# Laying a kernel's input by features and crossing its first four weight units

## The reference, cut to what matters

```python
def first_block(x, w_in, ...):
    proj = x @ w_in[l]                      # (256 x 1024) @ (1024 x 2560)
    q, k, v, g, p = jnp.split(proj, [...])  # 512 columns each
    q = _rope(q...)                         # rotation by position, on GpSimd here
    k = _rope(k...) * (RET_HEAD_DIM ** -0.5)
    ret = _retention(q, k, v)
    ...
    pool = _pool_mixer(p, w_pool[l], pool_scale[l])
    mix = jnp.concatenate([ret, pool], axis=-1) @ w_out[l]
    x = _layernorm(DEEPNORM_ALPHA * x + mix, ln1_g[l], ln1_b[l])
    ffn = _conv_ffn(x, ...)                 # 1024 -> 2 x 2816 -> 1024
    x = _layernorm(DEEPNORM_ALPHA * x + ffn, ...)
```

## Time and profile before

| | |
|---|---|
| median of the runs | 1067.66 us (1067.63 to 1068.27, 3 runs) |
| the profiled execution's own time | 1067.39 us |
| its span in the trace | 1065.4 us |
| PE busy | 1057.5 us (99%), 5158 matmuls |
| DVE, ACT, POOL busy | 738.0 us (69%), 596.5 us (56%), 96.5 us (9%) |
| moved by DMA | 227.13 MB, 213 GB/s on average |
| granted TensorE clock | 0.999 of full speed |

### The profile page before, as it was taken

The page is one execution under the profiler, slowest core; times in us unless marked ns, Lnnn a source line. Parts: engine busy times, 40 slices in busy tenths (PEclk is TensorE's granted clock), DMA queues, the critical chain, the costliest instruction groups (busy, mean ns, idle before and its releaser), DMA issues.

```text
span 1065.4 us, 13290 instructions
## 1 busy us (share of the span) xinstructions
PE 1057.5 (99%) x5158; PEld 890.2 (84%) x5158; DVE 738.0 (69%) x868; ACT 596.5 (56%) x804; POOL 96.5 (9%) x73
## 2 busy tenths in 40 slices
PE   9999999999999999999999999999999999999997
PEld 7888888888888888888888888888989988888886
DVE  6668777875786766467986768657568665867642
ACT  6463776764485645558655545464256557655531
POOL 2800000000000000000545500010000000000000
PEclk9999999999999999999999999999999999999999
DMA  9855999986588876475457844466556346777741
GB/s 357 301 171 170 302 282 293 306 265 197 180 269 244 246 246 227 158 242 171 160 164 215 249 145 158 138 239 218 180 178 214 119 139 210 238 245 241 243 166 40
DMA packets 152974, 227.13 MB, mean 213 GB/s; under 512 B 9376, under 2 KB 96336, under 8 KB 152784
## 3 DMA queue, kind: packets, MB, share of 16 engines
q1 hardware_dynamic: 149488, 214.86, 62.5%
q0 software_dynamic: 3136, 11.23, 3.1%
q10 hardware_dynamic: 288, 0.20, 0.1%
HBM read 211.57 MB, written 14.68 MB: 212 GB/s over the span
## 4 chain that ended last, share of the span: by engine, by line
PE 93%; DVE 3%; ACT 2%; issue 1%; DMA 0%; DVEq 0%; SPq 0%; ACTq 0%
PE ps L778 22%; PE ps L780 22%; PE ps L779 22%; PE ps L817 5%; PE ps L815 5%; PE ps L816 5%; PE ps L912 2%; PE ps L1237 1%; PE ps L1236 1%; PE ps L1235 1%; PE ps L1112 1%; DVE rest L1916 1%; PE ps L875 1%; PE ps L873 1%; PE ps L874 1%
## 5 line engine op out<-in xcount | busy, mean ns | idle before, releaser
L1916 DVE TENSOR_TENSOR rest<-raw,high 128x2048 fp32r<-128x2048 f32 x131 | 307.3, 2362 | 83.3 <-ACT high L1354 82.8
L778 PE MATMUL ps<-high,xt_high 128*128 128x512 f32 x840 | 330.5, 393 | 0.0
L780 PE MATMUL ps<-high,xt_rest 128*128 128x512 f32 x840 | 327.1, 389 | 0.0
L779 PE MATMUL ps<-rest,xt_high 128*128 128x512 f32 x840 | 327.0, 389 | 0.0
L1354 ACT ACTIVATE high<-raw 128x2048 fp32r<-128x2048 f32 x131 | 248.2, 1913 | 60.7 <-DMA raw<-in_ffn_w_down_dram 32.6
L780 PEld LDWEIGHTS ps<-high,xt_rest 128*128 128x128 f32 x840 | 157.7, 188 | 33.2
L779 PEld LDWEIGHTS ps<-rest,xt_high 128*128 128x128 f32 x840 | 157.9, 188 | 31.4
L778 PEld LDWEIGHTS ps<-high,xt_high 128*128 128x128 f32 x840 | 157.8, 188 | 31.2
L1921 DVE SCALAR_TENSOR_TENSOR rest<-raw,wgain,high 128x512 fp32r<-128x512 f32 x176 | 119.0, 746 | 36.0 <-ACT high L1358 36.0
L1358 ACT ACTIVATE high<-raw,wgain 128x512 fp32r<-128x512 f32 x176 | 110.8, 716 | 9.8 <-DMA raw<-in_ffn_w_in_dram 9.8
L1616 ACT ACTIVATE act<-ps,recips 128x256 f32<-128x256 f32 x44 | 18.4, 470 | 85.1 <-PE ps L780 85.0
(11 more groups left out here) (371 smaller groups left out, 1480.1 us busy)
## 6 DMA issues: line engine op xcount, KB each, us to landing
raw<-in_w_in_dram SPq DMA_DIRECT2D x88, 512.0 KB, 4.4
raw<-in_ffn_w_in_dram SPq DMA_DIRECT2D x88, 512.0 KB, 4.9
raw<-in_w_up_dram SPq DMA_DIRECT2D x44, 512.0 KB, 5.3
raw<-in_ffn_w_down_dram SPq DMA_DIRECT2D x44, 512.0 KB, 4.4
raw<-in_w_down_dram SPq DMA_DIRECT2D x22, 512.0 KB, 5.1
raw<-in_w_out_dram SPq DMA_DIRECT2D x16, 512.0 KB, 4.4
raw<-in_w_mkv_dram SPq DMA_DIRECT2D x16, 512.0 KB, 4.7
gv_turned<-gv_blocked SPq DMA_DIRECT2D x11, 512.0 KB, 7.0
```

The lines of the kernel that those rows point to most:

```text
L778: pe.matmul(out, sh, wh, start=first, stop=False)
L779: pe.matmul(out, sh, wr, start=False, stop=False)
L780: mm = pe.matmul(out, sr, wh, start=False, stop=last)
L1916: vec.tensor_tensor(rest[:, slot, c], raw[:, slot, c], high[:, slot, c].bitcast(F32), ALU.subtract).then_inc(unit_rest, 1)
```

## The change

The input is also handed over by features (`x_t`), so PE's sixteen transposes, and the ACT and DVE instructions that took them, are gone: ACT and DVE now split `xt_raw` directly, in five parts. Units 0 to 3 of `win1` hold the q and k blocks crosswise: unit 0 is q's first half, unit 1 k's first half, unit 2 and 3 their second halves, in twelve pieces that PE takes alternately from q and k for features 0 to 511, then q's rest, then k's. All weights are laid out on the host so that each DMA reads one unbroken piece of HBM (4 KB per partition, 2 KB for the first eight pieces); what the kernel loads into the slots is the same. `x` by tokens is loaded once, after unit 9. GpSimd's rotation tables wait for the eighth piece, its other constants for unit 4. PE's warming matmuls are seven, on a smaller tile. ACT issues the first part of `x_t` in place of `ident`, which follows later.

```diff
-WARM = (6, 4)
+WARM = 7
+LEAD_UNITS = 4
+XT_PARTS = ((0, 1), (1, 2), (2, 4), (4, 6), (6, 8))
+LEAD_PIECES = tuple((j, k, k + 1) for k in range(4) for j in range(2)) + tuple((j, k, k + 2) for j in range(2) for k in (4, 6))
...
+        def piece(name, c0, c1):
+            return dram[name][P * c0:P * c1].rearrange("(p n) -> p n", p=P)
...
+            def load_lead():
+                for n, (j, k0, k1) in enumerate(LEAD_PIECES):
+                    u = 2 * (k0 // 4) + j
+                    c = slice((k0 % 4) * NB, ((k1 - 1) % 4 + 1) * NB)
+                    for part, (x0, _) in enumerate(XT_PARTS):
+                        if part and j == 0 and x0 == k0:
+                            load_xt(part)
+                    at = u * 4 * NB
+                    sync.dma_start(raw[:, u, c], piece("units", at + c.start, at + c.stop)).then_inc(lead_landed[n], 16)
...
+            for u in range(LEAD_UNITS, UNIT["end"]):
+                load(u)
+                if u == UNIT["wout1"] - 1:
+                    sync.dma_start(x[:, :, :], dram["x"].rearrange("(t p) c -> p t c", p=P)).then_inc(x_landed, 16)
...
-            pool.wait_ge(unit_landed[3], 32)
+            pool.wait_ge(lead_landed[7], 16)
             for t, src in ((ropec, "c_ropec"), (ropes, "c_ropes")):
                 pool.dma_start(t[:], dram[src]).then_inc(rope_landed, 16)
+            pool.wait_ge(unit_landed[LEAD_UNITS], 32)
             for t, src in ((window, "c_window"), (decay, "c_decay"), (small["pscale"], "pool_scale")):
...
-            input_transposes(0)
-            warm(WARM[1])
-            wait_taken(("x", 0))
...
+            for n, (j, k0, k1) in enumerate(LEAD_PIECES):
+                u = 2 * (k0 // 4) + j
...
+                if n == 0:
+                    pe.wait_ge(xt_first, 1)
+                    pe.wait_ge(lead_high, 1)
+                    for tt in range(TT):
+                        xh, _, wh, _, out = lead(0, tt)
+                        pe.matmul(out, xh, wh, start=True, stop=False)
+                pe.wait_ge(lead_rest, n + 1)
+                if j == 0:
+                    pe.wait_ge(xt_rests, [part for part, (x0, x1) in enumerate(XT_PARTS) if x0 <= k0 < x1][0] + 1)
+                for k in range(k0, k1):
+                    for tt in range(TT):
+                        xh, xr, wh, wr, out = lead(k, tt)
+                        if n:
+                            pe.matmul(out, xh, wh, start=(k == 0), stop=False)
+                        pe.matmul(out, xh, wr, start=False, stop=False)
+                        mm = pe.matmul(out, xr, wh, start=False, stop=(k == KC - 1))
+                if k1 % 4 == 0:
+                    mm.then_inc(unit_used, 1)
+            full_block("win1", 2)
...
-            act.dma_start(small["ident"][:, :], dram["c_ident"]).then_inc(ident_landed, 16)
+            act.dma_start(xt_raw[:, 0, :], piece("x_t", 0, S)).then_inc(xt_landed[0], 16)
...
+            for n, (j, k0, _) in enumerate(LEAD_PIECES):
+                for part, (x0, _) in enumerate(XT_PARTS):
+                    if part and j == 0 and x0 == k0:
+                        input_high(part)
+                weights_high(n)
+            act.dma_start(small["ident"][:, :], dram["c_ident"]).then_inc(ident_landed, 16)
+            split[0] = LEAD_UNITS
...
+            vec.wait_ge(xt_landed[0], 16)
+            vec.tensor_copy(xt_high[:, 0, :], xt_raw[:, 0, :]).then_inc(xt_first, 1)
+            input_rest(0)
...
             split_to(UNIT["up1"] + 2)
+            vec.wait_ge(x_landed, 16)
             half_stats("wout1", 0, 0)
```

More of the change, by code:

```diff
@@ L541, in load @@
                     sync.wait_ge(unit_used, u - SLOTS + 1)
-                for dst, src in parts(raw[:, slot, :]):
-                    sync.dma_start(dst, src).then_inc(unit_landed[slot], 16)
+                for n in range(2):
+                    c = slice(2 * n * NB, 2 * (n + 1) * NB)
+                    sync.dma_start(raw[:, slot, c], piece("units", u * 4 * NB + c.start, u * 4 * NB + c.stop)).then_inc(unit_landed[slot], 16)
                 turn_conv(u)
@@ L936, in warm @@
                 for _ in range(n):
[L937 removed]
+                    pe.matmul(ps[:, 7, :], warmth[:, :], warmth[:, :].unsqueeze(1).to_broadcast([P, 4, P]), start=True, stop=True)
             pe.wait_ge(sem("warm_ready"), 1)
[L940 to L945 removed]
@@ L947, in _ @@
-            input_transposes(0)
-            warm(WARM[1])
-            wait_taken(("x", 0))
-            for tt in range(TT):
-                for k, (sh, sr, c, out, first, last) in enumerate(chunk_products("win1", 0, 0, tt)):
-                    if tt == 0:
-                        pe.wait_ge(*((sem("lead_rest"), k + 1) if k < 3 else (unit_rest, 1)))
-                    if (tt, k) == (0, 2):
-                        input_transposes(2)
-                    if (tt, k) == (0, 3):
-                        input_transposes(1)
-                    if (tt, k) == (1, 0):
-                        wait_taken(("x", 2))
-                    if (tt, k) == (1, 1):
-                        input_transposes(3)
-                    wh, wr = high[:, 0, c:c + NB], rest[:, 0, c:c + NB]
-                    pe.matmul(out, sh, wh, start=first, stop=False)
-                    pe.matmul(out, sh, wr, start=False, stop=False)
-                    mm = pe.matmul(out, sr, wh, start=False, stop=last)
@@ L966, in _ @@
-            mm.then_inc(unit_used, 1)
-            wait_taken(("x", 1), ("x", 3))
-            tiles = [chunk_products("win1", 0, 1, tt) for tt in range(TT)]
-            for k in range(4):
-                pe.wait_ge(*((sem("lead_rest"), k + 4) if k < 3 else (unit_rest, 2)))
-                for tt in range(TT):
-                    sh, sr, c, out, first, last = tiles[tt][k]
-                    wh, wr = high[:, 1, c:c + NB], rest[:, 1, c:c + NB]
-                    pe.matmul(out, sh, wh, start=first, stop=False)
-                    pe.matmul(out, sh, wr, start=False, stop=False)
-                    mm = pe.matmul(out, sr, wh, start=False, stop=last)
@@ L2667, in _, with in_pieces @@
             assert split[0] == UNIT["end"]
+def in_pieces(rows, ends):
+    return np.concatenate([rows[:, a:b].ravel() for a, b in zip([0] + list(ends), ends)])
 def constants():
```

210 lines of the change are left out of this document (91 added, 119 removed).

## The result

| | before | after |
|---|---|---|
| median of the runs | 1067.74 us (1067.63 to 1068.27, 5 runs) | 1072.12 us (1071.13 to 1074.45, 5 runs) |
| the profiled execution's own time | 1067.39 us | 1074.45 us |
| its span | 1065.4 us | 1072.3 us |
| first product | 6.53 | 4.48 |
| unit 4 (block p) starts | 30.12 | 28.17 |

The ratio after to before is 1.0042, with a 95% interval of 1.003 to 1.0053: slower by over 0.2%, and outside the range of 1064.0 to 1069.0. Two things make reading this kernel's trace harder than the one of before. Its executions lie 3.3 us apart where those of before lie 0.6 apart, and the profiled one is the slowest of them, so the profile shows 7.1 us of loss where the medians show 4.4.

A forecast was written before the change was run, and what follows sets the result against it. PE, busy 99% of the span, was taken as the bound. The opening's 3.4 us, less a new 2.4 us wait for GpSimd's rotation before k, left 1.0 us gained: 1066.5 us, range 1064.0 to 1069.0.

The forecast's parts named there:

- The start: First product on PE at 4.4 instead of 6.53, with a stall of 0.5 us before the third product.
- The opening: PE's q and k blocks before unit 4: ready for unit 4 at 26.7 instead of 30.12, 3.4 us won.
- PE runs on: After the third product, each 256 KB piece needs less time on DMA, ACT and DVE than PE's 1.36 us.
- When the first rotation starts: GpSimd begins its large constants about 20.3, spends 2.3 us on four issues, and rotates from 22.6.
- The insertions: DVE rests falling into GpSimd's rotations: three (units 4, 5, 7) at 2.0 us each, second rotation ending at 46.3.
- the gap of the DMA issues: GpSimd's DMA issues between the two rotations, where unit 6's rest was to fall.
- the rests get in at each boundary: Rival on GpSimd's rotations: four insertions give 1068.8 us, five 1070.8; chance 0.17, of it 0.10 with five.
- the undisturbed 17.7: Both GpSimd rotations without insertions, the four DMA issues between them included, take 17.7 us.
- At nothing: The other weights' layout, `x` after unit 9 and the later `ident` cost nothing; no PE wait ends in a DMA.
- 1.0 early: PE's transposes of k: wanted at 43.9, allowed at 46.35 after a 2.4 us wait, instead of 47.34.

The follow-up runs named there:

- e1: After, with eighteen matmuls of 512 columns that nothing reads put on PE before the transposes of k: 1069.21 us.
- e3: After, with ACT making the high part of unit 4 before it takes block q: 1069.78 us.
- e6: After, with the rests of units 4 to 8 computed on 512 of 2048 columns and the others set to zero by memset: 1069.6 us.
- e4: After, with GpSimd issuing the four small constants behind the rotation's tables instead of between its two rotations: 1070.61 us.
- e5: After once more, on another chip and with no edit: 1071.09 us.
- e9: After with the crossing undone, units 0 and 1 as q's halves and 2 and 3 as k's: 1067.03 us.
- e8: Before, with only the weight layout changed so every weight DMA reads an unbroken piece of HBM: 1067.4 us.
- e2: After with the rotation left out, one addition standing for its seven instructions for each of q and k: 1064.97 us.
- e7: After, with PE transposing k between the two halves of unit 7's matmuls: 1065.28 us.
- e11: After, with k transposed in the middle of unit 7 and unit 4's high part made before block q is taken: 1064.95 us.

## Why the prediction was wrong

*The start: right.* 4.48 for 4.4. The seven warming matmuls did not bring the pace up (the first two products stand 0.5 us apart), but the third product had its rest to wait for in any case and came at 5.47, forecast 5.4: that cost nothing, as I had it.

*The opening: 3.4 us forecast, 1.95 had.* The stall of 0.5 at the third product came as forecast. A second one, 0.95 us behind 7.57, was not in the sum: I had taken "PE runs on" for all later pieces from average rates of DMA, without asking when the third piece would land (7.32). Another 0.2 went before unit 4, 0.1 was the first product's start, and 0.2 lie scattered. Where the piece came in time (e1, e3, e6) 2.9 to 3.0 us were had. This made the gain smaller and, in after, the first rotation later.

*When the first rotation starts: 1.3 us off.* 23.87 for 22.6. The large constants were issued from 20.90 (forecast 20.3) to 23.25; the taking of q ended at 23.72 (22.4), and that was the later of the two. It followed the opening's second stall.

*The insertions: the step that failed.* The prediction's words were "three insertions (units 4, 5, 7), with unit 6 again in the gap of the DMA issues", on the ground that a rest directly behind another is passed over: unit 5's was to wait until the end of the first rotation and so keep unit 6's for the gap, unit 7's for the second rotation and unit 8's behind it. Unit 5's stood directly behind unit 4's and got in at the first boundary. Units 6 and 7 then entered the first rotation as well, and unit 8 the second: the sum of k ended at 51.7 instead of 46.3. The rival "the rests get in at each boundary", to which I gave 0.10 with five insertions (0.17 in all), has the second sum end at 50.4 from a start at 22.6 (its terms add up to 50.3); with the measured 23.87 that is 51.6, and 51.7 was measured. So the price of 2.0 us for each and the undisturbed 17.7 were right. The Trainium skill (SBUF — State Buffer, SBUF: two separate sides), whose exclusive lock by instruction I had cited for this rival, agrees with these rows. It also says that whoever starts first has the lock, and by e4, e5, e9 and the earlier trace rows that is not the whole of it: there GpSimd went on past a rest that was waiting.

*The clock behind the wait: not priced.* I charged a wait of PE at its length. 5.3 us of waiting cost 2.4 more in the matmuls behind it; e1 shows that this is the clock, since with PE kept busy they took 2.67 us. A forecast with all five insertions and without this term would still have been 2.4 us short.

*At nothing: right, but for the opening.* e8 for the layout; no PE wait after the opening ends in a DMA, in after or in any variant. The ground, that no PE wait ends in a DMA, did not hold inside it: the stall at 8.75 goes back to a landing.

*The ledger of the profiled execution.* Gained until unit 4, 1.95. Then k 4.42 late instead of 1.0 early, which is 5.4 us off: 1.3 of the rotation's start, 4.0 of two insertions more. Then 2.4 of the clock. Against the forecast of 1066.4 for a profiled execution, 1074.45 is 8.0 off; 5.4 and 2.4 are 7.8 of it. That is the slowest execution. For e5's, 1071.55, the same terms are 1.4 of the rotation's start and 2.0 of one insertion more, which is k at 49.84, and 1.6 of the clock: 1066.4 + 5.0 = 1071.4. So both steps stand in the milder case too.

*What the experiments bear out.* That the loss goes through GpSimd: e2, without the rotation, is faster than before by the opening's gain. That in after it reaches PE in one place: e7 and e11. (e4's edit moved it to unit 4.) What stays open is what decides between getting in and being passed over. So a forecast could price both cases, but not tell which comes.

## What to carry to other kernels

When two engines exclude each other instruction by instruction, work out the case in which every collision happens, and give it a large share unless a row shows what prevents it; one row in which it didn't happen is not a rule. Starting the matmuls earlier moves them onto the waits of the slow helper behind them: ask first what the helper's chain allows, and put work that doesn't need it in between (e7, 6 us) before saving anything on the chain. Price a new TensorE wait of some microseconds twice, at its length alone and with what would run at half clock behind it: here that added 1.3 to 3 us behind four waits of 2.8 to 5.3 us, and nothing behind one of 3.3.

## What the runs showed of the hardware

- DVE's subtraction of 128x2048 (2.29 us alone) and GpSimd's arithmetic never ran side by side; each rest that got in between two GpSimd instructions cost GpSimd 2.0 us, and one that had begun before GpSimd's first instruction cost it what was left of the rest (0.6 us in e11, 1.3 in e8). In the twelve profiles with both rotations and full rests (before among them), 40 rests met GpSimd with further instructions waiting: 32 got in at the first boundary, 8 were passed over at one to six. In e9 one was passed over although it began at 21.96 and GpSimd's first instruction at 22.71; in e11 one that began at 21.91, with GpSimd's at 23.44, was not. I found no rule.
- A memset of 128x1536 on DVE, with a short subtraction behind it, held GpSimd for 1.3 to 2.0 us in four places, and was not itself held (1.34 us each time, e6).
- The granted clock fell in waits of 5.3 us (after), 4.0 (e5, for a part of what followed), 3.6 (e4) and 2.8 (e6), but not in one of 3.3 (e3). The length of the wait alone doesn't decide it.
- The third piece of weights, 256 KB, issued at 2.12, landed at 7.32 in after, while 248 GB/s were moved on average over the first 8 us. With the same issues ahead of it ACT had it at 7.49 in e5 and at 6.37 in e1: landing times in the opening differ by 1 us between executions.
- The executions of after lie 3.3 us apart, those of before 0.6. In two of after's the order on the two engines differed by tenths of a microsecond and made 2.9 us; that this is the whole of the spread is not shown.
